# The second layer's values as a stage of their own, in two blocks of seven products, and the dense heads' value products inside a chunk

## The reference

```python
def second_block(x, w_in, w_out, t5_bias, na_rpb, ln_gain, ln_bias):
    h = x @ w_in                                   # 512 x 2048 @ 2048 x 8192
    qa, ka, va, ga, qb, kb, vb, gb = split(h)      # 16 dense heads, 16 neighbourhood heads, of 64
    ya = dilated_attention(qa, ka, va, t5_bias)    # three dilations, merged
    yb = neighbourhood_attention(qb, kb, vb, na_rpb)
    y = concat([ya * silu(ga), yb * silu(gb)])
    out = y @ w_out
    return layer_norm(ALPHA * x + out, ln_gain, ln_bias)
```

## Time and profile before

| | |
|---|---|
| three runs | 2477.97, 2478.79, 2479.11 us, median 2478.79 |
| span of the profiled execution | 2477.0 us; its own time is not listed apart, the median of the runs is 1.8 us above the span |
| TensorE busy | 2464.3 us, 99% |
| VectorE, ScalarE, GpSimd busy | 1506.1, 841.0, 696.6 us |
| granted TensorE clock | 0.999 |
| HBM read, written | 351.47 MB, 100.79 MB |

### The profile page before, as it was taken

How to read it: one execution, slowest core, us unless ns; L and a number is a source line. 1 busy time by engine, 2 the same in 40 slices (tenths; PEclk the granted TensorE clock), 3 DMA queues, 4 the chain that set the end, 5 groups by cost and what they waited for, 6 DMA issues and landing times.

```text
span 2477.0 us, 36169 instructions
## 1 busy us (share of the span) xinstructions
PE 2464.3 (99%) x13712; PEld 2092.3 (84%) x13712; DVE 1506.1 (61%) x2529; ACT 841.0 (34%) x1281; POOL 696.6 (28%) x867
## 2 busy tenths in 40 slices
PE   9999999999999999999999999999999999999998
PEld 7788899999988888888888888888888888888887
DVE  5664877898779976655554333556465545455525
ACT  7422444544454333333222222223232322223221
POOL 0312455666512222232001220211122334343100
PEclk9999999999999999999999999999999999999999
DMA  7748333433456766777544444676656555546622
GB/s 287 223 162 271 114 126 128 130 135 136 137 173 211 259 230 237 241 244 274 178 165 149 136 153 128 205 196 205 205 176 212 172 175 160 171 153 214 242 96 102
DMA packets 102405, 452.53 MB, mean 183 GB/s; under 512 B 18006, under 2 KB 18006, under 8 KB 74182
## 3 DMA queue, kind: packets, MB, share of 16 engines
q1 hardware_dynamic: 38712, 241.58, 28.7%
q0 software_dynamic: 63568, 209.25, 26.8%
HBM read 351.47 MB, written 100.79 MB: 183 GB/s over the span
## 4 chain that ended last, share of the span: by engine, by line
PE 98%; DMA 1%; SPq 0%; DVE 0%; ACT 0%; issue 0%; DVEq 0%
PE bank L456 23%; PE bank L457 22%; PE bank L458 22%; PE bank L874 16%; PE bank L1258 5%; PE bank L1181 2%; PE bank L1319 2%; PE bank L1160 2%; PE bank L1043 1%; PE bank L1018 1%; DMA w_raw<-wst 1%; PE bank L955 1%; PE bank L1038 0%; PE bank L1008 0%; PE bank L898 0%; PE bank L713 0%
## 5 line engine op out<-in xcount | busy, mean ns | idle before, releaser
L445 DVE TENSOR_TENSOR w_lo<-w_raw,w_hi 128x2048 fp32r<-128x2048 f32 x164 | 375.9, 2292 | 369.5 <-ACT w_hi L440 367.3
L456 PE MATMUL bank<-act_b,w_hi 128*128 128x512 f32 x1280 | 501.6, 392 | 0.0
L457 PE MATMUL bank<-act_b,w_lo 128*128 128x512 f32 x1280 | 498.4, 389 | 0.0
L458 PE MATMUL bank<-act_b,w_hi 128*128 128x512 f32 x1280 | 498.1, 389 | 0.0
L440 ACT ACTIVATE w_hi<-w_raw 128x2048 fp32r<-128x2048 f32 x163 | 311.7, 1913 | 509.6 <-PE bank L458 435.9
L456 PE MATMUL bank<-act_a,w_hi 128*128 128x512 f32 (+1 forms) x1032 | 405.8, 393 | 0.0
L457 PE MATMUL bank<-act_a,w_lo 128*128 128x512 f32 (+1 forms) x1032 | 401.9, 389 | 0.0
L458 PE MATMUL bank<-act_a,w_hi 128*128 128x512 f32 (+1 forms) x1032 | 401.8, 389 | 0.0
L456 PEld LDWEIGHTS bank<-act_b,w_hi 128*128 128x128 f32 x1280 | 240.2, 188 | 54.5 <-issue 5.2
L458 PEld LDWEIGHTS bank<-act_b,w_hi 128*128 128x128 f32 x1280 | 240.3, 188 | 50.4
L457 PEld LDWEIGHTS bank<-act_b,w_lo 128*128 128x128 f32 x1280 | 240.3, 188 | 48.8
(11 more groups left out here) (376 smaller groups left out, 3351.7 us busy)
## 6 DMA issues: line engine op xcount, KB each, us to landing
w_raw<-wst SPq DMA_DIRECT2D x210, 1024.0 KB, 5.0
prob_t<-flip_d POOLq DMA_DIRECT2D x64, 512.0 KB, 4.8
flip_d<-flip POOLq DMA_DIRECT2D x56, 512.0 KB, 4.3
mix_d<-stage POOLq DMA_DIRECT2D x24, 512.0 KB, 3.2
mixg<-mix_d POOLq DMA_DIRECT2D x8, 1536.0 KB, 6.8
prob_tk<-flip_d POOLq DMA_DIRECT2D x32, 256.0 KB, 6.0
flip_d<-flip_a POOLq DMA_DIRECT2D x16, 512.0 KB, 2.9
b<-rows_2d POOLq DMA_DIRECT2D x16, 448.0 KB, 10.3
```

The costliest lines, as they stand in the source:

```text
L445: dve.tensor_tensor(w_lo[s][:], w_raw[s][:], w_hi[s][:].bitcast(F32), ALU.subtract).then_inc(lo_ready, 1)
L456: pe.matmul(out_ap, l_hi, r_hi, start=start, stop=False)
L457: pe.matmul(out_ap, l_lo, r_hi, start=False, stop=False)
L458: return pe.matmul(out_ap, l_hi, r_lo, start=False, stop=stop)
```

## The change

- The second layer's values leave the steps. A stage of 32 chunks stands between `w_o` and the steps. The stationary operand is now x1 (tokens x features), the moved one 512 columns of weights, and so the values come out token-major. Two blocks (`sg` = 0, 1) of 1024 value columns each are computed by seven products of half size (256 tokens x 1024 features x 512 columns): a first phase of 8 chunks with three products (two blocks of x1 as they are, one sum of token blocks), and a second phase of 8 chunks with four (three sums of token blocks).
- GpSimd forms one sum of weight blocks per first-phase chunk and three per second-phase chunk (`value_sums`); ScalarE and VectorE split three or four parts of 512 columns (`value_hi`, `value_lo`). The chunks are loaded once for each phase: 768 KB for the first and 1 MB for the second.
- x1 is stored to `x1_d` as a whole, and the blocks that enter sums are loaded again (`tokens_load`, 8 loads of 512 KB). Sums of token blocks are on VectorE (`s1_sum`, `s2_sum`) and GpSimd (`s3_sum`, `s4_sum`), 4 x 256 columns at a time; each is split into a high and a low part. They are made once, during the first block, and serve both.
- The seven outputs are combined by ScalarE (`keep`), VectorE (`first_block_out`, `u2_out`, `u3_out`, `second_block_out`, `third_block_out`) and GpSimd (`fourth_sum`, `fourth_block`) and stored to `v2_d`, 16 stores a block.
- A step now has q and k over three chunks (1536, 1536 and 1024 columns) and the gate in a fourth of 2048, in a bank of its own. `v_to_tokens` only loads; VectorE's turn of v and GpSimd's four stores a step are gone.
- Dense heads' value products leave `beat`: tiles 2 and 3 of the pair before come ahead of chunk 1, tiles 0 and 1 behind the sixth k-tile of the gate chunk.
- y's first two parts are loaded when half of the last gate chunk is done (`gate_half`), not when the chunk before it is.

```diff
+        def v_phase(n):
+            return n // 16, n // 8 % 2, n % 8
+        V_PARTS = ((("raw", 0), ("raw", 2), ("sum", 0)), (("raw", 3), ("sum", 1), ("sum", 2), ("sum", 3)))
+        V_ORDER = ((0, 1, 2), (2, 0, 1, 3))
+        V_BANKS = (((4, 6, 0), (4, 6, 2, 0)), ((2, 4, 6), (2, 4, 0, 6)))
...
# SyncE
+            group_weights(G_IQ, G_V, CK * GC)
+            for sg in range(2):
+                group_weights(G_V + 8 * sg, G_V + 8 * sg + 4, 1536)
+                group_weights(G_V + 8 * sg + 4, G_V + 8 * sg + 8, CK * GC)
...
-            sp.wait_ge(chunk_used, 2 * G_OUT2 - 1)
+            sp.wait_ge(gate_half, GH0 + 16)
...
# TensorE
+            def value_chunk(n):
+                sg, ph, k = v_phase(n)
+                operands = ((act_b, k, 0), (act_b, k + 8, 0), (s1_x, k, 0)) if ph == 0 else \
+                           ((s4_x, k, 0), (s3_x, k, 0), (s2_x, k, 0), (act_b, k + 8, 256))
+                order = V_ORDER[ph]
+                for pos, i in enumerate(order):
+                    if i + 1 < len(order):
+                        pe.wait_ge(vp_lo, VL0 + parts_before(n) + i + 1)
+                    else:
+                        pe.wait_ge(lo_ready, 2 * G_V + n + 1)
...
+                    for t in range(2):
+                        for m, (l, r) in enumerate(((0, 0), (1, 0), (0, 1))):
+                            last = pe.matmul(v_bank(sg, ph, i, t), act[l][:, row, c0 + P * t:c0 + P * t + P], v_w[n % 2][i][r][:],
+                                             start=(k == 0 and m == 0), stop=(k == 7 and m == 2))
+                    last.then_inc(vp_used if pos + 1 < len(order) else chunk_used, 1)
...
-                if kind == "A2" and pair:
-                    for cc in range(2):
-                        pv2("A2", step, cc, par)
-                elif before == "A2" and pair == 0:
-                    for cc in range(2, 4):
-                        pv2("A2", step - 1, cc, 1 - par)
...
+                    if before == "A2" and cc == 1:
+                        for c in range(2, 4):
+                            pv2("A2", step - 1, c, 1 - par)
...
+                        for k in range(KT):
+                            if k == 6 and kind == "A2":
+                                for c in range(2):
+                                    pv2("A2", step, c, par)
+                            last = mm3(pe, bank[GATE_BANK][:], wt(w_hi[1], k, 0, P, P), wt(w_lo[1], k, 0, P, P),
+                                       act_b[0][:, k, :], act_b[1][:, k, :], start=(k == 0), stop=(k == KT - 1))
+                            if k == CK - 1:
+                                last.then_inc(gate_half, 1)
...
# VectorE, order of the first block
+            value_lo(0)
+            s1_sum(0)
+            tokens_lo(1, s1_x, s1_raw, 0)
+            value_lo(1)
+            x1_out_of(3, 1, last=True)
+            for n in range(2, 4):
+                value_lo(n)
+            value_lo(4, range(2))
+            s1_sum(1)
+            s2_sum(0)
+            tokens_lo(2, s1_x, s1_raw, 1)
+            value_lo(4, range(2, 3))
+            s2_sum(1)
+            value_lo(5)
+            tokens_lo(3, s3_x, s3_raw, 0)
+            value_lo(6)
+            tokens_lo(4, s2_x, s2_raw, 0, 2)
+            tokens_lo(5, s4_x, s4_raw, 0)
+            value_lo(7)
+            value_lo(8)
+            tokens_lo(6, s3_x, s3_raw, 1)
+            first_block_out(0)
+            value_lo(9)
+            tokens_lo(7, s2_x, s2_raw, 1, 4)
+            value_lo(10)
+            tokens_lo(8, s4_x, s4_raw, 1)
+            for n in range(11, 17):
+                value_lo(n)
+            u2_out(0)
+            u3_out(0)
+            second_block_out(0)
+            value_lo(17)
+            third_block_out(0)
...
# GpSimd
+            def value_sums(n):
...
+                jobs = ((t1, b12, b11, ALU.subtract),) if ph == 0 else \
+                       ((t3, b22, b12, ALU.subtract), (t2, t3[:], b11, ALU.add), (t4, t2[:], b21, ALU.subtract))
+                for i, (dst, l, r, op) in enumerate(jobs):
+                    if n:
+                        if ph == 0 or i == 2 or k == 0:
+                            pool.wait_ge(lo_ready, c)
+                        else:
+                            pool.wait_ge(vp_lo, VL0 + parts_before(n - 1) + i + 2)
...
+            value_sums(2)
             for s in range(2):
-                pool.wait_ge(x1_out[s], 416)
+                pool.wait_ge(x1_out[s], 464)
+            tokens_load(x_22, 12, 1, 1)
+            tokens_load(x_12, 12, 0, 3)
+            value_sums(3)
+            value_sums(4)
+            s3_sum(0)
+            value_sums(5)
+            s4_sum(0)
+            s3_sum(1)
+            value_sums(6)
+            s4_sum(1)
+            for n in range(7, 10):
+                value_sums(n)
+            v_store(v_u, 0, 0, (v_dve, VD0 + 2))
+            for n in range(10, 17):
+                value_sums(n)
+            fourth_sum(0)
+            value_sums(17)
+            fourth_block(0)
+            value_sums(18)
+            blocks_stored(0)
```

More of the change, by code:

```diff
@@ L1233, in _ @@
+                    last.then_inc(chunk_used, 1)
             pair_step(0, 1, None, None)
@@ new lines, in _ @@
+            tokens_hi(s4_x, s4_raw, 0, 3, 2)
+            value_hi(7)
+            value_hi(8)
+            tokens_hi(s3_x, s3_raw, 1, 4, 3)
+            keep(0, 0, v_p1, 0)
+            value_hi(9, range(2))
+            keep(0, 1, v_p5, 2)
+            value_hi(9, range(2, 4))
+            tokens_hi(s2_x, s2_raw, 1, 4, 3)
+            value_hi(10)
+            tokens_hi(s4_x, s4_raw, 1, 4, 4)
+            for n in range(11, 25):
+                value_hi(n)
+            keep(1, 0, v_p1, 0)
+            value_hi(25, range(2))
@@ L1704, in exp2 @@
+            keep(1, 1, v_p5, 2)
+            value_hi(25, range(2, 4))
+            for n in range(26, 32):
+                value_hi(n)
+            split_hi(act, 2 * G_IN2, 0, cols=PAIR_COLS[0])
             def exp2(kind, step, cc):
@@ new lines, in v_store @@
+            def v_store(src, row, col, done):
+                pool.wait_ge(*done)
+                for j in range(4):
+                    if col < 1024:
+                        at, step, block = 8 * row + j, 16, 4
+                    else:
+                        at, step, block = 256 * (j % 2) + 4 * row + j // 2, 8, 2
+                    pool.dma_start(bass.AP(v2_d, at * D + col, [[step * D, 32], [block * D, 2], [1, 512]]),
+                                   src[32 * j:32 * j + 32, :, :]).then_inc(v2_stored, 16)
```

530 lines of the change are left out of this document (382 added, 148 removed).

## The result

The changed kernel takes 2501.36 us, median of 4 runs (2500.16 to 2502.53), against 2478.95 us before in the same comparison: ratio 1.0093, 95% interval 1.0078 to 1.0107. It is slower by 22.4 us, where 2480.5 and no change were forecast. The profiled execution's span is 2498.6 us against 2477.0, so it shows 21.6 of them. The median of the kernel before was 2478.5 to 2478.8 in the comparisons further down; the new one's is not run again there, so its 2501.4 is carried over: of two kernels that differ by 3 us or less from different comparisons, the text says where their intervals overlap.

A forecast was written before the change was run, and what follows sets the result against it. TensorE was taken as the bound: 2477.0 - 21.8 + 14 + 2.5 + 1.5 + 0 + 5.4 = 2478.6 us, the median 1.8 above the span, so 2480.5 us and no change; 8-in-10 range 2463 to 2493.

The forecast's parts named there:

- What bounds it, and the products removed: Whole kernel: TensorE is the bound, so a waiting product is lost time; 96 products fewer save 21.8 us.
- Steady state: Value stage: helpers need 5.6 to 5.8 us per second-phase chunk against TensorE's 5.45; first-phase chunks have slack.
- The joint rate of 1.13: VectorE and GpSimd side by side: 7.5 us of lone work done in 6.6 us.
- The loop: Raw weight buffer, load to sums to low parts and again: 11.1 to 11.7 us per two second-phase chunks, against 10.9.
- I take 14: First value block, with token sums beside weight work: TensorE loses 14 us (0 to 22); its steps summed to 15.8.
- first loss: First block, chunk 4: x1's last tiles return late from store and load, costing about 2.5 us.
- a full lead: Second value block: double buffers give 6 to 8 us of lead, second-phase chunks eat 1 to 3; loss 1.5 (0 to 7).
- Between the blocks: Chunk 16's second product waits for banks the second output is read from: 2.5 us (0 to 4).
- The end: After the last pair: y loads lose cover, TensorE waits 3.1 us, then some 2.3; 5.4 us (3 to 6).
- Pairs at nothing: Shorter dense and neighbourhood pairs, 40.1 and 37.0 us, run without added waits: 0 us (0 to 8).
- the second, the port as the bound of the whole stage: Rival, value stage: VectorE and GpSimd share a port without overlap, 6.6 us per second-phase chunk; 2502 us, chance 0.25.
- The first rival: Value stage: the lead hides the new stage, first block loses 3 us, second 0; 2466.4 us, chance 0.33.

The follow-up runs named there:

- experiment 1: Changed kernel with SyncE reloading each raw weight buffer once its own readers are through, not after the chunk's last low part: 2498.72 us, ratio 1.0078.
- experiment 6: Changed kernel with weight sums on VectorE (2481.86 us), plus three unread GpSimd additions of 128 x 512 in each of chunks 24 to 30: 2501.56 us.
- experiment 4: Changed kernel with the weight sums of each chunk made by VectorE ahead of the low parts, not by GpSimd: 2481.86 us, ratio 1.0013.
- experiments 2: Changed kernel with x1's last four tiles read from the staging buffer for two token sums, not stored and loaded back: 2498.87 us, ratio 1.0083.
- experiment 5: Changed kernel with weight sums on VectorE and x1's last four tiles read from the staging buffer: 2480.80 us, ratio 1.0009.
- experiment 8: Changed kernel with the dense heads' value products back right behind the score products, not in mid-GEMM: 2540.71 us, ratio 1.0233.
- experiment 10: Changed kernel with all weight and token sums on VectorE, x1's last tiles from staging, earlier y loads; without moving dense value products 2473.47 us, with it 2503.66.
- experiment 3: Changed kernel without token loads, sums and splits, activation rows of the same shape taking their place (values wrong): 2483.98 us, ratio 1.0022.

## Why the prediction was wrong, by its own steps

- **What bounds it, and the products removed.** Right: every product that had to wait was lost time, and 96 went.
- **Steady state.** "5.8 us, or ... 5.6" for a second-phase chunk is what the helpers need, and experiment 1, where the loop is out of the way, runs at 5.66. The joint rate of 1.13 was read rightly too: in experiment 6 two operations of 1.98 us of lone work take 1.70, a rate of 1.16. (In the earlier trace rows GpSimd's last sum ends when nearer 1.7 than "about 1.3" of the next three low parts are made, which makes it 1.17.) The loop was put at "11.1 to 11.7 us for two chunks" and measured 12.28: the low part of the last sum takes 1.56 us, not 1.0, because the next chunk's first sum is beside it in the rows, and some 0.5 us pass between the steps.
- **The larger failed step: "I take 14" for the first block**, measured 23.8, above 22. The order was right: first loss at chunk 4, more to chunk 8, more to chunk 11; GpSimd's long sum is 2.40 us alone (experiment 4's trace), as taken. The helpers' work was nearly right as well. Chunk 11's last low part ends at 1571.04, 18.0 us after its due 1553.0 (1499.8 + 36.8 + 16.4), where the sum had 15.8. From chunk 4's third low part, ready at 1524.48, to there the 53.6 us of lone work (28.7 + 24.9) took 46.6, a joint rate of 1.15. The miss of 9.8 us is in what the sum left out. The term was set to 14, below its own 15.8, toward a joint rate of 1.25 that no row shows (1.8 us), and the helpers were later by 2.2. It counts the lateness at a chunk's last low part, but TensorE takes the second phase's parts in the order 2, 0, 1, 3 (`V_ORDER`) and so waits for the third low part before its first product:

```profile
1569.16 1.88 DVE L2652 TENSOR_TENSOR v_w<-v_sum,v_w 128x512 fp32r<-128x512 f32 x3
```

```profile
1570.49 0.50 PE L1285 MATMUL bank<-v_w,s_hi 128*128 128x512 f32 x1 [1.08 <-DVE v_w L2652]
```

Chunk 11 was due on TensorE at 1548.9 (1499.8 + 8 x 4.09 + 3 x 5.45) and starts at 1570.49, 21.6 us late: 3.6 more than by the last low part. And the sum ends at chunk 11, though chunks 11 to 15 lose 2.2 more at the helpers' pace. The 7.0 us of the store, where the earlier trace rows has 2.9, made little difference (experiments 2 and 5).

- **The other failed step: "a full lead is some 6 to 8 us; 8 second-phase chunks eat ... 1 to 3 us of it", so 1.5 us for the second block.** There was no full lead to eat. The second block began 2.4 us late. In its first phase and at its end the chain's loads took 4.7 and 5.3 us, and one 8.07 beside the value stores, where 3.8 was put, TensorE waited 1.20 and 0.86 us there and 2.17 at the first product of the second phase, and then eight chunks fell behind by 5.97 - 5.45 = 0.5 us each. Together 4.2 + 4.2 = 8.4 of the 9.6 us. The whole, 9.6, is above the upper bound of 7.
- **Between the blocks**: 2.5, measured 2.4. **The end**: 5.4, measured 4.4: the first wait is as forecast (3.1, measured 3.0); the second did not come, and the granted clock of 0.58 from 2310 to 2312 us accounts for part of the rest.
- **Pairs at nothing**: 3.8, inside the bound; the missing term is, by the rows of one pair, the turn between shapes. That nothing would wait for the probabilities was right, and only because the products were moved: experiment 8.
- **The rival that came nearest** is the second, the port as the bound of the whole stage, at 2502 us with a chance of 0.25. Its places are right: 22 us for the token stretch (21.6 to chunk 11), 13.6 for the second-phase chunks (2.2 + 9.6 = 11.8). But that its sum meets 2501.4 is in part luck: it has 4 between the blocks and 5.4 at the end, where 2.4 and 4.4 were measured, and nothing for the pairs, which took 3.8. Its condition, no overlap and 6.6 us a chunk, did not come, and its sign, "over 6 in the second block too", was just missed at 5.97. It "decides from 5.8 us a chunk on"; the forecast's own chunk was 5.6 to 5.8, and only the lead stood between the two. The first rival, at 0.33, rested on an average of the whole span and on a stage whose chunk lasts 10.1 us.

Open: how the 23.8 us divide among port, loop and clock, and why the first block is no shorter without the store. The experiments give 17 us to the token work, and about 5.6 us of the whole stage to the clock, from means with two digits.

## What to carry to other kernels

Before giving VectorE's work of two inputs to GpSimd, add up both engines' lone times per chunk and divide by the joint rate that a trace shows (here about 1.15): where that is above TensorE's time, the hand-over can cost instead of gain, and VectorE doing all of it can be faster (here 7 x 0.69 = 4.8 us instead of 6). Count lateness at the part that TensorE takes first, not at the last one made. A lead hides a shortfall only if an earlier phase has been seen to build it. When a stage gets shorter, look at every transfer that was hidden under it (probabilities, y tiles): the move that hides them again has its own price and may be what keeps the change from losing far more.

## What the runs showed of the hardware

- TensorE's granted clock fell to 0.50 right behind single waits: of 4.17 us (changed kernel), 4.30 (experiment 4), 4.50 (experiment 10) and 5.26 (experiment 6), and there products start 0.43 us apart. It was 0.50 behind one of 2.61 us in experiment 5 and 0.53 behind one of 1.93 in experiment 1, but 1.00 behind one of 2.37 in the changed kernel and of 3.22 in experiment 6, so the length of the wait alone does not tell.
- A store of 512 KB from SBUF landed after 2.9 us (before), 3.8 (experiment 3, without the token loads), 7.0 (changed kernel) and 11.0 (experiment 1, with earlier raw loads). What sets it was not tested.
- A turn of TensorE between the GEMM's products and the 128 x 64 value products costs 0.2 us there and back (starts 0.32 and 0.34 us apart instead of 0.23, changed kernel).
- VectorE's and GpSimd's additions of 128 x 512 with two inputs in SBUF, 0.69 and 1.29 us alone, take 1.70 us together when they alternate (experiment 6).
- GpSimd's copy of 128 x 512 (0.95 to 1.0 us) holds a two-input operation of VectorE up by some 0.3 us, its addition by 1.0.
